# Half-chunk products in a feed-forward down projection, and another order of the weight sums in the MLP's down sets, of a two-layer fp32 kernel

## The reference

```python
def _sq_relu_mlp(h, w_up, w_down):       # w_up 2048 x 8192, w_down 8192 x 2048
    a = jax.nn.relu(h @ w_up)
    return (a * a) @ w_down

def conv_ffn(hn, w_up, ffn_conv, w_down):    # w_up 2048 x 8192, w_down 4096 x 2048
    up = causal_dwconv(hn @ w_up, ffn_conv)
    gate, val = jnp.split(up, 2, axis=-1)
    return (jax.nn.silu(gate) * val) @ w_down
...
h = h + _sq_relu_mlp(_rmsnorm(h, mlp_norm[i]), mlp_w_up[i], mlp_w_down[i])
...
h = h + conv_ffn(rmsnorm(h, norm_ffn[l]), w_up[l], ffn_conv[l], w_down[l])
```

## Time and profile before

| what | value |
| --- | --- |
| median of 3 runs | 2473.53 us (2472.73 to 2474.16) |
| the profiled execution: time | 2473.63 us |
| its span, first to last instruction | 2471.8 us |
| outside the span | 1.8 us |
| PE (matmul) busy | 2459.8 us, 100% |
| PEld (weight load) busy | 2030.9 us, 82% |
| DVE busy | 1660.3 us, 67% |
| ACT busy | 1608.6 us, 65% |
| DMA, read over the span | 468.33 MB, 190 GB/s |

### The profile page before, as it was taken

How to read it: one execution, slowest core, us unless ns; L and a number is a source line. 1 busy time by engine, 2 the same in 40 slices (tenths; PEclk the granted TensorE clock), 3 DMA queues, 4 the chain that set the end, 5 groups by cost and what they waited for, 6 DMA issues and landing times.

```text
span 2471.8 us, 29802 instructions
## 1 busy us (share of the span) xinstructions
PE 2459.8 (100%) x12367; PEld 2030.9 (82%) x12367; DVE 1660.3 (67%) x1371; ACT 1608.6 (65%) x2119; POOL 33.4 (1%) x41
## 2 busy tenths in 40 slices
PE   9999999999999999999999999999999999999998
PEld 7887788888888888888888888888888888888887
DVE  5865658787778868577764785545666677646675
ACT  6545778856748658776465684545586788638873
POOL 0000000000000000000000000000000000000000
PEclk9999999999999999999999999999999999999999
DMA  8554556545554555545443445555655555555554
GB/s 289 187 190 168 173 188 237 190 181 208 206 203 178 215 207 188 189 171 198 158 149 140 157 174 195 196 188 197 261 189 176 192 194 188 199 191 190 200 189 153
DMA packets 69366, 472.36 MB, mean 191 GB/s; under 512 B 7912, under 2 KB 8352, under 8 KB 13424
## 3 DMA queue, kind: packets, MB, share of 16 engines
q1 hardware_dynamic: 67040, 460.62, 51.5%
q0 software_dynamic: 1312, 7.73, 0.8%
q10 hardware_dynamic: 880, 2.11, 0.2%
HBM read 468.33 MB, written 2.11 MB: 190 GB/s over the span
## 4 chain that ended last, share of the span: by engine, by line
PE 93%; DVE 2%; ACT 2%; issue 1%; DMA 1%; SPq 0%; POOLq 0%; POOL 0%; DVEq 0%; ACTq 0%
PE acc L615 28%; PE acc L617 28%; PE acc L616 28%; DMA w_raw<-in_stream 1%; PE tp L759 1%; PE tp L758 1%; PE tp L757 1%; ACT w_hi L1198 1%; DVE w_lo L1874 1%; PE acc L757 1%; PE acc L759 1%; PE acc L758 1%; ACT sq L1391 1%; PE tp L979 1%; PE tp L912 0%
## 5 line engine op out<-in xcount | busy, mean ns | idle before, releaser
L1874 DVE TENSOR_TENSOR w_lo<-w_raw,w_hi 128x2048 fp32r<-128x2048 f32 x416 | 950.9, 2288 | 616.4 <-ACT w_hi L1198 614.2
L1198 ACT ACTIVATE w_hi<-w_raw 128x2048 fp32r<-128x2048 f32 x416 | 795.6, 1915 | 394.3 <-DMA w_raw<-in_stream 346.8
L615 PE MATMUL acc<-w_hi,x_hi 128*128 128x512 f32 (+1 forms) x2112 | 826.2, 391 | 1.4 <-DVE w_lo L1881 0.6
L617 PE MATMUL acc<-w_hi,x_lo 128*128 128x512 f32 (+1 forms) x2112 | 819.7, 388 | 0.0
L616 PE MATMUL acc<-w_lo,x_hi 128*128 128x512 f32 (+1 forms) x2112 | 819.5, 388 | 0.0
L615 PEld LDWEIGHTS acc<-w_hi,x_hi 128*128 128x128 f32 x2112 | 396.8, 188 | 86.8 <-issue 2.9
L617 PEld LDWEIGHTS acc<-w_hi,x_lo 128*128 128x128 f32 x2112 | 396.7, 188 | 81.3
L616 PEld LDWEIGHTS acc<-w_lo,x_hi 128*128 128x128 f32 x2112 | 396.9, 188 | 80.3 <-issue 1.0
L615 PE MATMUL acc<-w_hi,a_hi 128*128 128x512 f32 x1024 | 400.0, 391 | 0.4 <-DVE w_lo L1874 0.2
L616 PE MATMUL acc<-w_lo,a_hi 128*128 128x512 f32 x1024 | 399.0, 390 | 0.0
L617 PE MATMUL acc<-w_hi,a_lo 128*128 128x512 f32 x1024 | 398.9, 390 | 0.0
(11 more groups left out here) (482 smaller groups left out, 1954.2 us busy)
## 6 DMA issues: line engine op xcount, KB each, us to landing
w_raw<-in_stream SPq DMA_DIRECT2D x416, 1024.0 KB, 4.8
w_raw<-in_stream SPq DMA_DIRECT2D x16, 256.0 KB, 8.2
raw_T<-in_stream SPq DMA_DIRECT2D x4, 1024.0 KB, 7.2
raw_b<-in_stream SPq DMA_DIRECT2D x4, 1024.0 KB, 8.9
raw_t<-in_stream SPq DMA_DIRECT2D x3, 1024.0 KB, 7.0
raw_d<-in_stream SPq DMA_DIRECT2D x3, 1024.0 KB, 10.2
h<-in_x SPq DMA_DIRECT2D x4, 512.0 KB, 14.0
frow<-in_rows POOLq DMA_DIRECT2D x2, 1024.0 KB, 6.5
```

The costliest lines, as they stand in the source:

```text
L615: pe.matmul(dst, xh, wh[:, k], start=first and k == 0, stop=False)
L617: mm = pe.matmul(dst, xl, wh[:, k], start=False, stop=last and k == n_k - 1)
L1198: act.activation(w_hi[:, c % SLOTS], raw(c), ACT.Copy).then_inc(hi_ready, 1)
L1874: dve.tensor_tensor(low_part(c), raw(c), w_hi[:, c % SLOTS].bitcast(F32), ALU.subtract).then_inc(lo_ready, 1)
```

## The change

It does two things.

**In the feed-forward's first part** the down projection's column blocks 2 and 3 take seven products for eight too. down_pair now takes its first step, its accumulators, the pair of u tensors and two semaphore counts, and is called with step C_FFN + 13, so that the steps 27 to 37 of the MLP are the steps 40 to 50 of this part, which gets 51 steps instead of 48. ffn_pair on DVE forms the sums f1 to f4 and the differences uf_raw; two pieces (f3 and f22) are loaded besides. The eight chunks at the end of the part (192 matmuls) become four chunks and seven products (180).

**In the MLP's down sets** the weight sums are formed from other operands and at other steps. Before: t3 = B12 + B22 at step 23, t1 and t2 from it with B11 at step 24. Now: t1 = B11 + B12 at step 24, t3 at step 25, t2 = t1 + d22 at step 26. u_lo moves from step 25 to step 24, behind that step's split.

frow2, the final gain, is now loaded by the POOL queue only after the first part.

```diff
-    PAIRS = GROUPS + 3
+    PAIRS = GROUPS + 4
...
+        F_PART = [C_FFN, C_FFN + 51]
+        assert F_PART[1] + 48 == NITEM
...
+        FFN_SUM_AT = {29: "f22", 31: "f1", 32: "f2", 35: "f3", 36: "f4"}
...
+                if c == C_FFN + 36:
+                    sp.dma_start(sum_raw["f3"][:], stream[ffn_chunk(0, 3)]).then_inc(b12_in, 16)
+                    sp.wait_ge(g_tanh, 4)
+                    sp.dma_start(sum_raw["f22"][:], stream[ffn_chunk(1, 3)]).then_inc(b22_in, 16)
...
+            pool.wait_ge(used, F_PART[1])
             pool.dma_start(frow2[:], rows[:, N + D:N + 2 * D]).then_inc(row2_in, 16)
...
+                    if g == 0 and c == 40:
+                        down_pair(C_FFN + 13, accs.name["fdown", 0, 2], accs.name["fdown", 0, 3], (uf_hi, uf_lo), 10, 15)
+                    if c >= (40, 45)[g]:
                         break
...
+                    if part == 0 and c == 37:
+                        act.wait_ge(s_formed, 9)
+                        act.activation(uf_hi[:].rearrange("p s k t -> p (s k t)"), uf_raw[:].rearrange("p s k t -> p (s k t)"), ACT.Copy).then_inc(pair_out, 1)
...
-                if c == 23:
-                    dve.wait_ge(b12_in, 32 * part + 32)
-                    dve.wait_ge(b22_in, 32 * part + 32)
-                    dve.wait_ge(sq_moved, 4 * part + 4)
-                    dve.tensor_tensor(sum_raw["t3"][:], sum_raw["t1"][:], sum_raw["d22"][:], ALU.add).then_inc(sum_ready, 1)
                 if c == 24:
                     b11 = weights_in(27)
+                    dve.wait_ge(b12_in, 32 * part + 32)
+                    dve.wait_ge(sq_moved, 4 * part + 4)
+                    dve.tensor_tensor(sum_raw["t1"][:], b11, sum_raw["t3"][:], ALU.add).then_inc(sum_ready, 1)
+                if c == 25:
+                    dve.wait_ge(b22_in, 32 * part + 32)
+                    dve.tensor_tensor(sum_raw["t3"][:], sum_raw["t3"][:], sum_raw["d22"][:], ALU.add).then_inc(sum_ready, 1)
+                if c == 26:
+                    dve.wait_ge(a_low, 4 * part + 4)
                     dve.wait_ge(sum_ready, 8 * part + 5)
-                    dve.tensor_tensor(sum_raw["t1"][:], sum_raw["t1"][:], b11, ALU.add).then_inc(sum_ready, 1)
-                    dve.wait_ge(a_low, 4 * part + 4)
-                    dve.tensor_tensor(sum_raw["t2"][:], sum_raw["t3"][:], b11, ALU.add).then_inc(sum_ready, 1)
+                    dve.tensor_tensor(sum_raw["t2"][:], sum_raw["t1"][:], sum_raw["d22"][:], ALU.add).then_inc(sum_ready, 1)
...
-                if c == 25:
+                if c == 24:
                     dve.wait_ge(pair_out, pair_step(part, "s"))
                     dve.tensor_tensor(u_lo[:], u_raw[:], u_hi[:].bitcast(F32), ALU.subtract).then_inc(s_formed, 1)
...
+            def ffn_pair(c):
...
+                if c == 35:
+                    for q in range(2):
+                        ins = dve.tensor_tensor(vf_sum[:, q], a_hi[:, 4 * q:4 * q + 4].bitcast(F32), a_lo[:, 4 * q:4 * q + 4].bitcast(F32), ALU.add)
+                    link(ins)
+                if c == 36:
+                    dve.wait_ge(nat_turned, 16 + 8)
+                    dve.tensor_tensor(uf_raw[:, 2], rows_[0][0], rows_[1][0], ALU.subtract)
...
+                if c == 37:
+                    b11 = weights_in(40)
+                    dve.wait_ge(b12_in, 16 * 8)
+                    dve.wait_ge(sq_moved, 16 + 8)
+                    dve.tensor_tensor(sum_raw["f1"][:], b11, sum_raw["f3"][:], ALU.add).then_inc(sum_ready, 1)
+                if c == 38:
+                    dve.wait_ge(b22_in, 16 * 8)
+                    dve.tensor_tensor(sum_raw["f3"][:], sum_raw["f3"][:], sum_raw["f22"][:], ALU.add).then_inc(sum_ready, 1)
+                    dve.wait_ge(pair_out, 1 + 6 * 3 + 5 + 1)
+                    dve.tensor_tensor(uf_lo[:], uf_raw[:], uf_hi[:].bitcast(F32), ALU.subtract).then_inc(s_formed, 1)
+                if c == 39:
+                    dve.wait_ge(f_taps, 8)
+                    dve.wait_ge(sum_ready, 4 * 7 + 1)
+                    dve.tensor_tensor(sum_raw["f2"][:], sum_raw["f1"][:], sum_raw["f22"][:], ALU.add).then_inc(sum_ready, 1)
...
```

More of the change, by code:

```diff
@@ L146, in build @@
             sum_lo[t] = sb(f"lo_{t}", [P, CH], F32R, a_sum[t])
+        a_sum.update({"f1": a_s + 24 * K, "f2": a_s + 32 * K, "f3": a_s + 16 * K, "f4": a_s + 8 * K, "f22": a_s + 8 * K})
+        for t in ("f1", "f2", "f3", "f4", "f22"):
+            sum_raw[t] = sb(f"raw_{t}", [P, CH], F32, a_sum[t])
+            sum_lo[t] = sb(f"lo_{t}", [P, CH], F32R, a_sum[t])
+        vf_sum = sb("vf_sum", [P, 2, 4, SEQ], F32, a_sh)
+        uf_hi = sb("uf_hi", [P, 4, 4, P], F32R, a_sh)
+        uf_raw = sb("uf_raw", [P, 4, 4, P], F32, a_nat)
+        uf_lo = sb("uf_lo", [P, 4, 4, P], F32R, a_nat)
         v_sum = sb("v_sum", [P, 2, 4, SEQ], F32, a_nat)
@@ L457, in source @@
                 return i
+            if i >= F_PART[1]:
+                return i - 3 * PAIRS
+            if i >= C_FFN and i - C_FFN - 13 in DOWN_AT:
+                return ffn_chunk(*DOWN_AT[i - C_FFN - 13])
             if i >= C_2:
-                return i - 3 * PAIRS
+                return i - 3 * (PAIRS - 1)
             g, k = divmod(i - C_MLP, GROUP)
@@ L794, in up_pair, with down_pair @@
                 chunk(c0 + 18, X, 12, right, False, True)
-            def down_pair(g):
-                c0, left, right = C_MLP + GROUP * g, accs.name["down", g, 2], accs.name["down", g, 3]
+            def down_pair(c0, left, right, u, formed, taken):
                 chain, both = tpf(0)[:, 0:N], tpf(0)[:, N:2 * N]
@@ L837, in _ @@
                 if g < 3:
-                    down_pair(g)
+                    pe.wait_ge(pair_out, pair_step(g, "p7"))
+                    down_pair(C_MLP + GROUP * g, accs.name["down", g, 2], accs.name["down", g, 3], (u_hi, u_lo), 2 * g + 4, 5 * g)
             def mats(hf):
@@ L1807, in _ @@
             for part in range(2):
-                for c in range(48):
+                for c in range((51, 48)[part]):
                     b, q = divmod(c, 4)
@@ L1833, in _ @@
                     if not (q == 1 and 1 <= b <= 8):
-                        split(C_FFN + 48 * part + c + AHEAD)
+                        split(F_PART[part] + c + AHEAD)
                     if q == 2 and b in (1, 3, 5, 7):
@@ L2674, in other_taps, with weights_in @@
                 return ins
+            def ffn_pair(c):
+                left, right = [slice(n * N, (n + 1) * N) for n in (2, 3)]
+                chain, both = tpf(0)[:, 0:N], tpf(0)[:, N:2 * N]
+                rows_ = [[vf_sum[:, q, :, m * P:(m + 1) * P] for q in range(2)] for m in range(M)]
+                def weights_in(k):
+                    dve.wait_ge(landed[PLACE[C_FFN + k] % SLOTS], landing(PLACE[C_FFN + k]))
+                    return raw(C_FFN + k)
+                if c == 35:
[5 more added lines that the diff above has]
+                    dve.tensor_tensor(uf_raw[:, 2], rows_[0][0], rows_[1][0], ALU.subtract)
+                    link(dve.tensor_tensor(uf_raw[:, 0], rows_[1][0], rows_[1][1], ALU.subtract))
+                    link(dve.tensor_tensor(uf_raw[:, 1], uf_raw[:, 0], rows_[0][0], ALU.subtract))
+                    dve.tensor_tensor(uf_raw[:, 3], uf_raw[:, 1], rows_[0][1], ALU.add).then_inc(s_formed, 1)
+                if c == 37:
[12 more added lines that the diff above has]
+                    dve.tensor_tensor(sum_raw["f2"][:], sum_raw["f1"][:], sum_raw["f22"][:], ALU.add).then_inc(sum_ready, 1)
+                if c == 42:
+                    dve.wait_ge(used, C_FFN + 41)
+                    dve.tensor_tensor(h[:, 0, left], chain, h[:, 0, left], ALU.add).then_inc(down_out, 1)
+                    b21 = weights_in(46)
+                    dve.wait_ge(used, C_FFN + 43)
+                    dve.wait_ge(sum_ready, 4 * 7 + 3)
+                    dve.tensor_tensor(sum_raw["f4"][:], sum_raw["f2"][:], b21, ALU.add).then_inc(sum_ready, 1)
+                if c == 46:
+                    dve.wait_ge(used, C_FFN + 46)
+                    dve.tensor_tensor(h[:, 0, right], h[:, 0, right], chain, ALU.subtract).then_inc(down_out, 1)
+                    dve.wait_ge(down_out, 15 + 2)
+                    dve.tensor_tensor(h[:, :, right], h[:, :, right], both.unsqueeze(1).to_broadcast([P, M, N]), ALU.add).then_inc(down_out, 1)
+                if c == 49:
+                    dve.wait_ge(used, C_FFN + 49)
+                    dve.tensor_tensor(h[:, 1, left], chain, h[:, 1, left], ALU.add).then_inc(down_out, 1)
+                    dve.wait_ge(down_out, 15 + 3)
+                    dve.tensor_tensor(h[:, 1, right], h[:, 1, right], chain, ALU.subtract).then_inc(down_out, 1)
+                if c == 50:
+                    dve.wait_ge(down_out, 15 + 4)
+                    add_to_h(("fdown", 0, 2), 2, C_FFN + 49)
+                    dve.wait_ge(down_out, 15 + 5)
+                    add_to_h(("fdown", 0, 3), 3, C_FFN + 50)
@@ L2679, in _ @@
```

(4 more changed lines are left out.)

42 lines of the change are left out of this document (22 added, 20 removed).

## The result

| kernel | median | runs |
| --- | --- | --- |
| before | 2473.58 us | 2472.69 to 2474.53, 9 |
| changed | 2480.19 us | 2478.94 to 2480.73, 9 |

What follows compares the result with a forecast made beforehand. The matmul engine was taken to bound the kernel, busy 2459.8 of 2471.8 us. 2473.63 + 6.60 (down sets) - 2.72 (fewer matmuls) + 0.15 (hitches) = 2477.66, forecast as 2477.6 us, range 2475.3 to 2480.0.

Steps and rivals of the forecast that it cites:

- Part 1, the MLP's sets: MLP's three down sets: split 28, and PE's step 28 with it, come 2.20 us later in each, +6.60 us.
- The hole: DVE's idle time ahead of split 26, waiting for ACT; with t3 taken out of it, about 3.9 us.
- the sum: Whole kernel: 2473.63 + 6.60 - 2.72 + 0.15 = 2477.66 us, forecast as 2477.6 for the median.
- the two hitches: Feed-forward, pieces 41 and 42: leads of 0.2 and 0.1 us give two short PE halts, +0.15 us.
- the clock: Rival, down sets: TensorE's clock halves in the longer halts, 16.3 us more, 2493.9 us; chance 0.03.
- Part 2, the feed-forward: Feed-forward's first part: 12 matmuls fewer, -2.72 us if PE runs without a halt; DVE's and ACT's added work nearly hidden.
- The late chain: Rival, feed-forward: DVE's splits come late and PE halts; one instruction's time, 2.20 us, gives 2479.8 us; chance 0.14.
- the new order could be free: Rival, down sets: split 26 starts 2.2 us earlier, so no delay; 2470.8 us, or 2469.2 without old halts; chance 0.09.
- The sign of the loss: Whole kernel: 0.16% slower, within the about 0.2% a measurement can tell; slower by over 0.2% had chance 0.24.

Runs made afterwards that it cites:

- E5: The changed kernel with u_lo formed in two halves, one on each side of split 28: 2477.41 us, 1.0017 of before.
- E1: The changed kernel with the MLP's down sets in the old order of sums, the feed-forward's seven products kept: 2470.73 us, 0.9990 of before.
- E4: The changed kernel, but ACT rounds piece 26 ahead of u_hi in step 23 of the down sets: 2469.03 us, 0.9984 of before.
- E8: The changed kernel with the old order of sums and ACT rounding piece 26 ahead of u_hi: 2468.81 us, 0.9981 of before.

## Why the prediction was wrong, by its steps

**Part 1, the MLP's sets: right in mechanism and size.** The hole was foreseen at 3.9 us and is 3.78; split 28 was to be 2.20 us later and is 2.21. The distances of "about 2.7 us" are 2.54 to 2.95. E5, whose halts add up to about the same and whose clock doesn't fall, stands at 2477.41; the sum without the two hitches gives 2477.4 for the median.

**The step that failed is the clock.** The sum priced a halted microsecond as a microsecond, and the forecast went by that; the clock was put aside as a rival with a chance of 0.03, for the reason that gaps of 0.5 us had not moved it. That row had nothing to say on gaps of 2.5 us, as the prediction itself said, so no row stood behind the 0.03. I also priced the rival as all or nothing, 5.44 us in each of three sets, 16.3 in all. It is neither: in the executions profiled with halts of this length it falls in one or two sets of three, takes about 1.6 us each time, and makes up most of the 2.8 us (2.5 by each group's own runs of before) between the medians of E5 and of the changed kernel. The term was missing from the sum, and the upper end of the range, 2480.0, lay 0.2 us too low. The prediction had named a granted clock under 1.00 in the MLP as a sign of being wrong, and this is the sign that came.

**Part 2, the feed-forward: right, with a lead underestimated.** The 12 matmuls gave 2.72 us in the trace, and E1 alone 2.3 us in the medians, within its interval (0.2 to 4.7 us less than before). The 0.15 us for two hitches wasn't there. I had ACT starting on piece 37 8.17 us behind its issue, as in the MLP; it was issued at 2136.18 and ACT started 6.8 us later, so its rounding was done at 2144.93, ahead of the place where DVE wanted it. ACT and DVE in the changed kernel:

```profile
2143.01 1.92 ACT L1224 ACTIVATE w_hi<-w_raw 128x2048 fp32r<-128x2048 f32 x1 [2.46 <-DMA w_raw<-in_stream]
```

```profile
2145.73 2.28 DVE L1903 TENSOR_TENSOR w_lo<-w_raw,w_hi 128x2048 fp32r<-128x2048 f32 x1
...
2168.47 2.28 DVE L1903 TENSOR_TENSOR w_lo<-w_raw,w_hi 128x2048 fp32r<-128x2048 f32 x1
...
2174.01 2.28 DVE L1903 TENSOR_TENSOR lo_f<-raw_f,w_hi 128x2048 fp32r<-128x2048 f32 x1
```

From 2145.73 on DVE goes through without a delay. Split 41 ends at 2170.75 and PE wants it at 2171.34; lo_f22 ends at 2176.29 and is wanted at 2176.78. The lead is 0.6 and 0.5 us, not 0.2 and 0.1.

**The rivals.** The late chain did not come about in the feed-forward. That the new order could be free was wrong as the change stands, but what it named as the condition, ACT's rounding of piece 26 out of the 5 us of waiting ahead of u_hi, is the edit of E4, and it removes the halts. I had named 2469.2 us for that case; E4 took 2469.03.

**The sign of the loss.** I expected a loss of 0.16%, within what can be told, and gave 0.24 to one beyond it. It is 0.26%, interval 0.16 to 0.36.

## What to carry to other kernels

An instruction that stands in a hole, where its engine must wait for another one anyway, is free, and the same instruction behind the wait costs its full time if the engine is already the one that others wait for: read the order of an engine between a wait and the piece that is wanted, not its busy share. The hole itself can be the thing to mend: here ACT waited 5 us with work at hand that DVE needed, and swapping two of its instructions made both orders of the sums fast. A halt of TensorE of a few microseconds can cost more than its length: here two of 1.4 to 1.7 us, from start to start, were cheaper by some 2.5 us over three sets than one of 2.5 to 3 us in each.

## What the runs showed of the hardware

The clock of TensorE fell behind six of twelve halts with start distances of 2.44 to 2.95 us, behind none of seven from 1.39 to 2.02, and behind all three over 5. It fell behind one of 2.44 us and not behind one of 2.90. Behind the six it gave seven or eight matmuls at 0.42 to 0.43 us, some 1.6 us lost each. E5 and the changed kernel have nearly the same DVE work and nearly the same sum of halts, and differ by 2.8 us (2.5 by each group's own runs of before).

The order of the three instructions of equal length, t3, u_lo and t2, made no difference that the runs can tell where the hole was closed (E4 and E8, 0.2 us apart, 0.5 by their groups' own runs of before), although it moved the time by 9 us where it was open.
